# Sums of squares and one mask level moved from VectorE to ScalarE in a two-block transformer kernel

## What is computed

```python
# first block
mod = silu(c) @ w_ada + b_ada                      # six sections of 2048: shift1, scale1, gate1, shift2, scale2, gate2
h = rms_norm(x) * (1 + scale1) + shift1            # 1/sqrt(mean(x*x) + 1e-6) per row
aq, ak, av, gq, gf, gi, gg = split(h @ w_in)       # 1024 columns each
attn = rms_norm(dilated_attention(rope(aq), rope(ak), av))     # 8 heads of 128
hg = rms_norm(hgrn2(gq, gf, gi), per head) * silu(gg)          # gated recurrence, 8 heads of 128
x = x + gate1 * (concat(attn, hg) @ w_out)
h2 = rms_norm(x) * (1 + scale2) + shift2
x = x + gate2 * (relu(h2 @ w_ff1) ** 2 @ w_ff2)
# second block
x = x + stick_breaking_attention(rms_norm(x) @ w_qkv) @ w_o
x = x + relu(rms_norm(x) @ w_in2) ** 2 @ w_out2
```

## Time and profile before

| what | value |
|---|---|
| runs, us | 2454.43, 2456.74, 2457.46 |
| median | 2456.74 us |
| span of the profiled execution | 2453.7 us |
| time of the profiled execution outside its span | not recorded by itself; the median is 3.0 us above the span |
| TensorE busy (matmul) | 2362.5 us, 96% |
| VectorE busy | 1593.8 us, 65% |
| ScalarE busy | 1036.6 us, 42% |
| mean granted TensorE clock | 0.990 of full speed |

### The profile page before, as it was taken

How to read it: one execution, slowest core, us unless ns; L and a number is a source line. 1 busy time by engine, 2 the same in 40 slices (tenths; PEclk the granted TensorE clock), 3 DMA queues, 4 the chain that set the end, 5 groups by cost and what they waited for, 6 DMA issues and landing times.

```text
span 2453.7 us, 27892 instructions
## 1 busy us (share of the span) xinstructions
PE 2362.5 (96%) x10954; PEld 1969.7 (80%) x10954; DVE 1593.8 (65%) x1282; ACT 1036.6 (42%) x874; POOL 47.8 (2%) x55
## 2 busy tenths in 40 slices
PE   4899999988999999999999999999999999999999
PEld 3777888777888888888887888878888888888887
DVE  7878989966566666656568556556555555555554
ACT  2255553434333333343344556664443333333432
POOL 1011000000000000000000000000000000000000
PEclk9999999999999999999999999999999999999999
DMA  9988997653677667655554645435555555555553
GB/s 352 371 295 319 354 318 273 224 175 117 224 242 243 234 229 238 225 193 176 188 189 142 219 155 161 164 124 168 184 188 187 191 193 185 191 188 188 188 188 103
DMA packets 235129, 520.30 MB, mean 212 GB/s; under 512 B 9705, under 2 KB 10162, under 8 KB 232370
## 3 DMA queue, kind: packets, MB, share of 16 engines
q1 hardware_dynamic: 234352, 519.15, 62.7%
q10 hardware_dynamic: 706, 0.17, 0.0%
HBM read 517.19 MB, written 2.10 MB: 212 GB/s over the span
## 4 chain that ended last, share of the span: by engine, by line
PE 88%; DVE 5%; DMA 2%; ACT 2%; issue 1%; DVEq 1%; POOL 1%; ACTq 0%; SPq 0%
PE PS L256 27%; PE PS L258 27%; PE PS L257 27%; DMA ada_raw<-in_w_ada_dram 2%; PE PS L1599 2%; PE PS L1638 1%; DVE w_lo L246 1%; DVE ada_acc L1096 1%; PE PS L1573 1%; PE PS L303 1%; ACT w_hi L242 1%; POOL rstd L570 1%; PE PS L1583 1%; ACT A_hi L339 0%; DVE MS L1041 0%
## 5 line engine op out<-in xcount | busy, mean ns | idle before, releaser
L246 DVE TENSOR_TENSOR w_lo<-raw,w_hi 128x2048 fp32r<-128x2048 f32 x392 | 897.8, 2291 | 698.2 <-ACT w_hi L242 692.7
L242 ACT ACTIVATE w_hi<-raw 128x2048 fp32r<-128x2048 f32 x392 | 751.6, 1918 | 1170.7 <-PE PS L258 1158.8
L256 PE MATMUL PS<-w_hi,A_hi 128*128 128x512 f32 x2112 | 838.7, 397 | 9.9 <-DVE A_lo L358 5.4
L258 PE MATMUL PS<-w_hi,A_lo 128*128 128x512 f32 x2112 | 827.6, 392 | 0.0
L257 PE MATMUL PS<-w_lo,A_hi 128*128 128x512 f32 x2112 | 827.5, 392 | 0.0
L256 PEld LDWEIGHTS PS<-w_hi,A_hi 128*128 128x128 f32 x2112 | 400.2, 190 | 92.6 <-DVE A_lo L358 5.0
L258 PEld LDWEIGHTS PS<-w_hi,A_lo 128*128 128x128 f32 x2112 | 399.7, 189 | 84.4
L257 PEld LDWEIGHTS PS<-w_lo,A_hi 128*128 128x128 f32 x2112 | 400.2, 190 | 81.5 <-issue 1.0
L256 PE MATMUL PS<-w_hi,H_hi 128*128 128x512 f32 x1024 | 401.6, 392 | 1.6 <-issue 1.3
L258 PE MATMUL PS<-w_hi,H_lo 128*128 128x512 f32 x1024 | 398.9, 390 | 0.0
L257 PE MATMUL PS<-w_lo,H_hi 128*128 128x512 f32 x1024 | 398.4, 389 | 0.0
(11 more groups left out here) (265 smaller groups left out, 1111.7 us busy)
## 6 DMA issues: line engine op xcount, KB each, us to landing
raw<-in_w_ff_dram SPq DMA_DIRECT2D x128, 1024.0 KB, 5.3
raw<-in_mlp_w_in_dram SPq DMA_DIRECT2D x64, 1024.0 KB, 5.5
raw<-in_mlp_w_out_dram SPq DMA_DIRECT2D x64, 1024.0 KB, 5.0
raw<-in_w_in_dram SPq DMA_DIRECT2D x56, 1024.0 KB, 8.2
X<-in_w_ada_dram SPq DMA_DIRECT2D x96, 512.0 KB, 5.7
raw<-in_sb_w_qkv_dram SPq DMA_DIRECT2D x48, 1024.0 KB, 5.1
ada_raw<-in_w_ada_dram SPq DMA_DIRECT2D x32, 1024.0 KB, 9.8
raw<-in_w_out_dram SPq DMA_DIRECT2D x16, 1024.0 KB, 7.4
```

Of the source, the lines that this page charges most:

```text
L242: act.activation(w_hi[:, j, :, :], raw[:, j, :, :], ACT.Copy).then_inc(hi_rdy, 1)
L246: dve.tensor_tensor(w_lo[:, j, :, :], raw[:, j, :, :], w_hi[:, j, :, :].bitcast(F32), ALU.subtract).then_inc(lo_rdy, 1)
L256: pe.matmul(bank(pair + t), h, w_hi[:, j, k, :], start=first, stop=False)
L258: mm = pe.matmul(bank(pair + t), l, w_hi[:, j, k, :], start=False, stop=last)
```

## The change

Five things are done differently. The sums of squares of x, of the attention half of `MIX`, and of the first three output blocks are made by ScalarE, as a `Square` activation with a row sum (`accum_out`); VectorE waits for a new semaphore `row_sq` where it used the sums. The ones for the fourth output block and for all later norms stay on VectorE. The level of width 16 leaves `LEVELS`: VectorE makes no mask for it and doesn't copy it, and ScalarE's `wide_copy` takes it (for width 16 it runs four copies, of 16 partitions each). With `NFINE` one smaller, TensorE waits for `lv_wide` where it waited for `lv_cp` ahead of the level of width 32.

```diff
-LEVELS = (1, 2, 4, 8, 16)
+LEVELS = (1, 2, 4, 8)
...
@@ scalar program
+            act.wait_ge(x_in, 16)
+            act.wait_ge(ssq_set, 1)
+            for t in range(T):
+                act.activation(Y0[:, t, :], X[:, t, :], ACT.Square, accum_out=ssq[:, t:t + 1]).then_inc(row_sq, 1)
             act.wait_ge(rstd_rdy, POWER_OF[0])
             for c in range(4):
                 normalise(act, X, X, c)
...
                     (hg_own if kind == "hg" else at_own)(idx, B0, s)
+                    if kind == "hg" and idx == 0 and s == 12:
+                        act.wait_ge(hg_tr, 1)
+                        for t in range(T):
+                            act.drain()
+                            act.activation(QN[:, :, :].rearrange("p t n -> p (t n)"), MIX[:, t, 0:AW], ACT.Square,
+                                           accum_out=ssq[:, t:t + 1]).then_inc(row_sq, 1)
                     split_hi(act, B0 + s // CH + 1, s % CH)
...
+            def block_squares(b):
+                act.wait_ge(x_add, b + 1)
+                for t in range(T):
+                    act.drain()
+                    act.activation(E0f[:, 0:NC_], X[:, t, NC_ * b:NC_ * (b + 1)], ACT.Square,
+                                   accum_out=ssq_blocks[:, b, t:t + 1]).then_inc(row_sq, 1)
...
             for pos in range(OUT_EARLY, CH * 4):
                 split_hi(act, OUT0 + 1 + pos // CH, pos % CH)
+                if pos >= CH * 4 - 5 and pos < CH * 4 - 2:
+                    block_squares(pos - CH * 4 + 5)
@@ vector program
-            dve.memset(ssq[:, :], 1.0)
+            dve.memset(ssq[:, :], 1.0).then_inc(ssq_set, 1)
...
-                dve.wait_ge(x_in, 16)
-                for t in range(T):
-                    dve.tensor_tensor_reduce(Y0[:, t, :], X[:, t, :], X[:, t, :], 1.0, 0.0, ALU.mult, ALU.add,
-                                             ssq[:, t:t + 1])
-                d()
+                dve.wait_ge(row_sq, T)
...
-                            dve.wait_ge(hg_tr, 1)
-                            for t in range(T):
-                                d()
-                                dve.tensor_tensor_reduce(QN[:, :, :].rearrange("p t n -> p (t n)"), MIX[:, t, 0:AW],
-                                                         MIX[:, t, 0:AW], 1.0, 0.0, ALU.mult, ALU.add, ssq[:, t:t + 1])
+                            dve.wait_ge(row_sq, 2 * T)
                             rsqrt(dve, T, 1.0 / AW, EPS)
...
-                dve.tensor_tensor(xs, xs, VN[:, :, :], ALU.add)
-                block_squares(b)
+                dve.tensor_tensor(xs, xs, VN[:, :, :], ALU.add).then_inc(x_add, 1)
                 d()
...
+            dve.wait_ge(row_sq, 2 * T + 3 * T)
             root_of_blocks()
```

More of the change, by code:

```diff
@@ L207, in build @@
         ring_used, sel_rdy, mod_mm, mod_rdy = (sem(n) for n in ("ring_used", "sel_rdy", "mod_mm", "mod_rdy"))
-        sum_rdy, rstd_rdy = sem("sum_rdy"), sem("rstd_rdy")
+        sum_rdy, rstd_rdy, row_sq, x_add, ssq_set = sem("sum_rdy"), sem("rstd_rdy"), sem("row_sq"), sem("x_add"), sem("ssq_set")
         y_rdy, x_done, row_rdy = sem("y_rdy"), sem("x_done"), sem("row_rdy")
```

## The result

The changed kernel took 2471.38 us (median of four runs, 2468.05 to 2472.32), the kernel before 2456.38 us. The ratio is 1.0057, 95% interval 1.0044 to 1.0070: 15 us slower where I had forecast 0.3 us faster. The profiled execution of the changed kernel has a span of 2468.5 us, 14.8 us above that of before.

The account below looks back on a forecast made before the run. TensorE, busy 96% of the span, was taken to bound the kernel, the start being bound by transfers and `ada_raw` slots. Places gave -0.3 + 0 + 0 + 0: span 2453.4, time 2456.4 us, range 2453.0 to 2458.6.

Parts of the forecast that it names:

- the list of what the change takes and gives: Work moved between engines: 15.5 us taken from VectorE, 0.6 us of it for the mask; 12.4 us given to ScalarE.
- Place 1, first norm: Squares of x at the start: VectorE goes on 0.7 us earlier (bounds 0.2 to 0.9), kernel gains 0.3 us.
- Three signs that I had named: Expected scaling of `ssq` at 28.1 to 28.9; failure signs: `AM` wait below 4 us, weight-chunk start moved over 1 us.
- Rivals 1 and 4: First norm slower: table load for `Square`, 2457.3, chance 0.03; dearer row sums or semaphore hop, about 2457.4, chance 0.09.
- Place 2, mix norm: Squares of `MIX` fit ScalarE's 2.62 us gap ahead of `split_hi`; VectorE gains 2.7 us, TensorE none.
- Place 3, level 16: Recurrent groups: VectorE's saved copies become longer waits; ScalarE's four copies, 1.5 us, fit 3.7 us of slack; gain 0.
- rival 3: TensorE's width-32 level waits for ScalarE's four strided PSUM copies: 5 us slower, 2461.7, chance 0.04.
- Place 4, output blocks: VectorE's 4.8 us become a longer wait; ScalarE's pairs of squares fit a 3.52 us gap; kernel gains 0.
- The last step of the sum: From predicted span 2453.4 us to forecast time 2456.4 us, by the runs' median lying 3.0 us above the profiled span.
- Rival 2: VectorE's pace holds TensorE's chunks, so all 15.5 us come off: 2441.2, chance 0.06.

## Why the prediction was wrong

**The step that failed** is the list of what the change takes and gives, and with it the sum, which let the time move only through waits between engines. The list counted the level's mask as 0.6 us of VectorE's work and left out that it is also 128 bytes of memory, from which the place of every later tile follows. So the sum had four places and lacked a fifth: 3072 down matmuls at +5.4 ns, 16.6 us in the trace, for which it had nothing. The filler tiles' names and sizes stood in the code, and the declaration of `lv_mask` with `len(LEVELS)` in it is in the same list of tiles. None of the four rivals had this mechanism; those that ended slower (1, 3 and 4) did so for other reasons.

**Place 1, first norm**: right in kind, too small. ScalarE's squares in the changed kernel, and VectorE behind them:

```profile
23.93 1.91 ACT L755 ACTIVATE raw<-X 128x2048 f32<-128x2048 f32 x1 [9.42 <-DMA X<-in_x_dram]
25.74 0.19 ACT L755 ACTIVATION_READ_ACCUMULATOR raw<-X 128x1 f32 x1
25.83 1.89 ACT L755 ACTIVATE raw<-X 128x2048 f32<-128x2048 f32 x1
27.63 0.19 ACT L755 ACTIVATION_READ_ACCUMULATOR raw<-X 128x1 f32 x1
```

```profile
27.85 0.17 DVE L992 TENSOR_SCALAR ssq<-ssq 128x2 f32<-128x2 f32 x1 [4.19 <-ACT raw L755]
```

A row sum is an instruction of 0.19 us, 0.1 us of it under the next pass. VectorE goes on at 27.85 instead of 29.07: 1.2 us, above my upper bound of 0.9, because x landed 0.3 us sooner and the passes overlap. The transfers from 31 to 40 us ran at 406 GB/s against 341 in the earlier trace rows:

```profile
31.00:40.00 9.00, 4.85 (x23) 4.85 (x23) 6.28 (x3) 5.01 (x8) 0.81 (x1) 1.00 1.03 406
```

TensorE's first weight chunk starts at 78.23 instead of 79.28 (chain of either kernel), 1.05 us earlier where I had taken 0.3. One pair of traces is weak evidence, but all fifteen kernels point the same way. The three with these squares on ScalarE ran at 396 to 406 GB/s in that window and started the chunk at 77.97 to 78.23; the twelve with them on VectorE ran at 320 to 346 GB/s and started it at 78.06 to 79.80, 79.1 on average. So the slots given back earlier were worth about 1 us here, not half of 0.7. By the turn of `ACC` it can't be told from the scatter any more (594.65 to 596.68 in the three), and the median of the runs doesn't show it. Three signs that I had named were touched, none with an effect on the time: the scaling came before 28.1, the start moved by over 1 us, and the wait for `AM` is 4.0 us, at the edge of "below 4". No new table load stands ahead of the Squares. Rivals 1 and 4 did not happen.

**Place 2, mix norm**: as predicted. Two squares of 1.06 us and two sums fill the gap ahead of `split_hi`, and VectorE's scaling comes at 333.68 instead of 337.17.

```profile
329.67 1.06 ACT L780 ACTIVATE QN<-MIX 128x1024 f32<-128x1024 f32 x1
```

```profile
333.68 0.17 DVE L377 TENSOR_SCALAR ssq<-ssq 128x2 f32<-128x2 f32 x1
```

**Place 3, level 16**: as predicted. The four copies take 1.09 us, 0.26 each where I allowed 0.37. VectorE's next step waits 2.27 us instead of 0.30 for TensorE, and in the second group 5.39 instead of 3.98: what was saved has become waiting, and rival 3's wait does not exist.

```profile
393.94 1.09 ACT L643 ACTIVATE AM<-PS 16x128 f32<-16x128 f32 x4
```

```profile
401.11 0.69 DVE L1165 TENSOR_TENSOR bT<-bT,MIX 128x512 f32<-128x512 f32 x1 [2.27 <-PE PS L1649]
...
515.50 0.69 DVE L1165 TENSOR_TENSOR bT<-bT,MIX 128x512 f32<-128x512 f32 x1 [5.39 <-PE PS L1649]
```

**Place 4, output blocks**: as predicted. A pair of squares lies in ScalarE's gap, of which 1.91 of the 3.52 us of the earlier trace rows are left, and TensorE's 6.5 us wait for `ACC` is unchanged.

```profile
568.54 0.63 ACT L803 ACTIVATE E<-X 128x512 f32<-128x512 f32 x1
...
569.88 0.19 ACT L803 ACTIVATION_READ_ACCUMULATOR E<-X 128x1 f32 x1
571.98 1.92 ACT L242 ACTIVATE w_hi<-raw 128x2048 fp32r<-128x2048 f32 x1 [1.91 <-PE PS L258]
```

**The last step of the sum**, from the span to the time, used 3.0 us, the median of the runs less the span of another execution. The profiled execution of the changed kernel took 2470.51 us for a span of 2468.5 us, so 2.0 us would have been right; this 1 us decides nothing.

**Rival 2** (all of it counts) did not happen: with the places restored, 14.4 us less of VectorE's work give a ratio of 0.9999.

## What to carry to other kernels

Read a diff for memory as well as for work: a constant that sizes a tile moves every tile behind it. Where a kernel keeps fillers between its tiles, work out the distances of the operands of its matmuls before and after, and mend the filler in the same edit. And where time is lost in a stage that the diff doesn't touch, compare the mean of one matmul by its operands before looking for a wait: 5 ns on each of 3072 outweighed everything else here.

## What the runs showed of the hardware

The pace of float32 matmuls of 128x512, each with a freshly loaded 128x128 operand, depends on where the stationary and the moving tile lie against each other in SBUF, modulo 256 bytes. At a distance of 0 modulo 256 the starts of consecutive down matmuls lie 227 ns apart in the trace, at 128, with all of them off, 232 to 233 ns, and at 64 they lie 228 to 230 ns apart. The mean durations follow, group by group: for the three down matmuls from 392, 389 and 390 ns to 398, 394 and 395; for the matmuls with `A_hi` or `A_lo` from 397, 392 and 392 to 401, 396 and 396. End to end that is 14.8 us for 3072 matmuls (4.8 ns each), 27.8 us for 6336 (4.4 ns) and 40.1 us for all 9408 (4.3 ns); at 64 it was 6.3 us for 3072 (2.0 ns). Moving both operands together costs nothing (1.0006, interval 0.9996 to 1.0015). The clock was granted in full from 700 to 1250 us and from 1800 to 2400 us, in the two MLPs, in the trace of every kernel here, and the loads of the down projection's stationary tiles kept a mean of 188 to 189 ns (191 in one group of the run with `H_lo` off), so it isn't either of these.

The Trainium skill, page "SBUF — State Buffer", section "Operand start alignment", asks of an operand's start only a multiple of its element size and says that this is about legality, not speed. The runs agree that all these places are legal, and show that they differ in speed.

What stays open is how it comes about. A distance from start to start grows when just one of the two neighbours is out of step, on either side, so a price that each matmul pays for its own tile alone doesn't fit. Nor does a fixed price for each distance: it is 5.6 ns in some and 7.7 ns in others, and `H_hi` alone off costs more than both tiles off. I didn't try distances other than 64, 128 and 256, nor other shapes or types.
